# Normalizing the head outputs instead of the softmax rows, and adding the sample's value pages on GpSimd

## The chip, the cores and the metric

The kernel runs on one core of a Trainium2 chip. The metric is the time on the device of one execution, in microseconds (us). Before the change it was 2890.0 us as the median of three runs, from 2884.14 to 2896.01. Engines are called PE (TensorE), DVE (VectorE), ACT (ScalarE), POOL (GpSimd) and SP (SyncE, which issues most of the DMAs).

## The reference, cut to what matters

A two-layer decoder of width 1024 is run for a prompt of 1024 tokens and for 8 sample rows of one token each, in float32: a gated short convolution and a SwiGLU FFN, then one shared K and V with a log-forget value per head, then attention with 16 heads of 64, its output projection and a second FFN. Only the attention is touched:

```python
def _attend(q, k, v, cum_q, cum_kT, q_pos):
    s = jnp.einsum("bqhd,bkhd->bhqk", q, k).astype(jnp.float32) * ATTN_SCALE
    s = s + jnp.swapaxes(cum_q, 1, 2)[..., None] - cum_kT[:, :, None, :]
    k_pos = jnp.arange(k.shape[1])
    s = jnp.where(k_pos[None, :] <= q_pos[:, None], s, -jnp.inf)
    p = jax.nn.softmax(s, axis=-1).astype(v.dtype)
    return jnp.einsum("bhqk,bkhd->bqhd", p, v)
```

For the prompt, q, k and v have 1024 positions. For the samples there is one query per row, and the keys and values are 512 past positions, gathered as four pages of 128 positions out of a pool, and the new one.

## The kernel before, in words

Every engine has its own program, written out by hand, and every order and wait in it is explicit. A float32 operand of a product is kept as a high part (fp32r) and a low part, and a product is two or three matmul passes.

The prompt's attention is done in pairs of heads: 8 pairs, numbered b, and 8 steps in a pair, st 0 to 7, four for each of its two heads e. A step has 256 query rows as two tiles t of 128, and j = st mod 4 says how far down the sequence they are: `span(st, t)`, the width in keys, is 128*(2j+t+1), and `width(st)` is j+1 groups of 256 keys. The work of a step is a pipeline over the engines:

- PE `scores` (L2385, L2388, with a mask pass L2387): q times k-high and k-low into PSUM banks 0 to 3.
- DVE `maxima` (L1953): adds the forget bias, writes the scores to `ss[j]` in SBUF and gives the row's extreme.
- ACT `exps` (L1360): exponential in place, with the row sum. DVE `inverse` (L1961): `ri` = 1 / row sum.
- POOL `norm` (L910): multiplies both tiles of `ss[j]` by `ri`, in place.
- PE `turn` (L2403): transposes the tiles, 128 by 128, into PSUM bank 4 or 5; ACT `pt_high` (L1367) and DVE `pt_low` (L1966) take the high and low part out, group by group.
- PE `values` (L2419, L2420): v times the transposed weights into bank 6 or 7. ACT `o_take` (L1380) copies the result to `oe[e]`, whose two halves of 64 rows belong together.
- When a head is done, SP's `store_head` (L623) writes one half to DRAM (`o_t`), and POOL's `add_halves` (L916) waits for that to land and adds the other half to it by an accumulating DMA.

On PE, step st does `turn` of st, `scores` of st+3 and `values` of st-1. The loop body over b has steps 2 to 9, and steps 8 and 9 are steps 0 and 1 of the next pair. In the last pair, `o_half` (ACT) and `o_sum` (DVE, L1978) add the halves in SBUF.

Loads for the next pair are issued by SP: `load_qk` (L574, L578, L579: q, k, forget bias; `next_qk`), `load_v` (L583; `next_v`). POOL's `k_split` (L899, L901) makes k-high and k-low of a head, and `scores` of that head's first step waits for it. POOL's queue in the body is: norm 4, k_split of the next pair's head 0, norm 5 to 7, add_halves 0, norm 8, k_split of head 1, norm 9 to 11, add_halves 1. SP's is: next_qk 0, value pages 2 and 3, next_qk 1, next_v 0, store_head 0, the next sample's pages 0 and 1, next_v 1, store_head 1.

There are as many samples as pairs of heads, and sample b's past values are summed in pair b. SP loads a page of `cache_v` (L611, 128x1024, two buffers `vp`), and PE's `sample_page` (L2433, at the end of steps 2, 4, 6 and 8) takes the page as weights, eight blocks, against two columns of the sample's softmax weights `pst`. DVE's `sample_sum` (L2003) adds the four pages' results.

Of the kernel before, what the change touches and what calls it, by code (L numbers as in the profile page):

```python
# [62 lines left out]
SCOL = 256  # L63
HIST = 2
# [102 lines left out]
def build(nc, a):  # L167
    ctx = ExitStack()
    with ctx:
# [16 lines left out]
        class Area:  # L186
# [5 lines left out]
            def put(self, name, shape, dt):  # L192
# [128 lines left out]
        vp = Area(Z_END).put("vp", [P, 2, D], F32)  # L321

# [70 lines left out]
              ("khi", "klo", "sfull", "sdr", "exp", "rinv", "pnorm", "tfull", "pthi", "ptlo", "ofull", "ohalf", "odone")}  # L393
# [4 lines left out]
               "pt", "pst", "pe", "o", "osum", "done")}  # L398
# [31 lines left out]
        def _(sp):  # L430
# [256 lines left out]
        def _(pool):  # L687
# [215 lines left out]
            def norm(b, st):  # L903

                j = st % STEPS
                inverted = pool.to_reg(PAIR * b + st + 1) if not isinstance(b, int) else PAIR * b + st + 1
# [15 lines left out]
            norm(0, 0)  # L922
            sample_rows_out()
            k_split(0, 1)
            for st in range(1, STEPS):
                norm(0, st)
            for m in range(WR):
                low(SLOTS["o"] + m, SLOTS["o"] + m)
            with pool.Fori(0, KB - 1) as b:
# [29 lines left out]
        def _(act):  # L959
# [410 lines left out]
            def o_take(b, st):  # L1370

                e, j = st // STEPS % 2, st % STEPS
                act.wait_ge(at["ofull"], PAIR * b + st + 1)
                if j == 0:

                    act.wait_ge(oe_add[e], 16 * (b + st // PAIR + 1))
                if st == 1:

                    act.wait_ge(sm["osum"], b + 1)
                act.activation(oe[e][:, j * 2 * P:(j + 1) * 2 * P], ps[:, 6 + st % 2, 0:2 * P], ACT.Copy).then_inc(at["odone"], 1)  # L1380
# [36 lines left out]
            for st in range(2, PAIR):  # L1417
                step(KB - 1, st, True)
            o_half(PAIR - 2)

            act.wait_ge(sm["o"], NS * PPB + 2)
# [57 lines left out]
        def _(dve):  # L1479
# [490 lines left out]

            def o_sum(st):
# [6 lines left out]
                dve.tensor_tensor(ost[e * DH:(e + 1) * DH, j * 2 * P:(j + 1) * 2 * P], ps[0:DH, 6 + st % 2, 0:2 * P],  # L1978
                                  otmp[:, st % 2, :], ALU.add).then_inc(at["odone"], 1)

            def step(b, st, last=False):


                for g in range(STEPS):
                    if g < width(st):
                        pt_low(b, st, g)
                    if g in (1, 2) and not (last and st + 3 >= PAIR):
                        maxima(b, st + 3, g - 1)
                if not (last and st + 2 >= PAIR):
                    inverse(b, st + 2)  # L1990
                if last and st >= 2:
                    o_sum(st - 2)

            def sample_sum(b):

                paged = dve.to_reg(PPB * b + PPB + 2) if not isinstance(b, int) else PPB * b + PPB + 2
                apart(dve)
                dve.wait_ge(sm["o"], paged)
                taken = dve.to_reg(2 + PAIR * (b + 1)) if not isinstance(b, int) else 1 + PAIR * (b + 1)
                dve.wait_ge(at["odone"], taken)  # L2000
                for t in range(2):
                    rows = slice(t * DH, (t + 1) * DH)
                    last = dve.tensor_reduce(opast[rows, bass.ds(b, 1), :].rearrange("p a k -> p (a k)"),  # L2003
                                             ps[rows, 7, SCOL:SCOL + PPB * H].rearrange("p (g k t) -> p t k g", g=PPB, t=2)[:, t],
                                             AX, ALU.add)
                last.then_inc(sm["osum"], 1)
# [59 lines left out]
        def _(pe):  # L2066
# [303 lines left out]
            def scores(b, st, t):  # L2370
# [7 lines left out]
                if not (isinstance(b, int) and b == 0 and st == 0):  # L2378
                    pe.wait_ge(at["sdr"], 2 * s - 2 + t + 1)
                q = qa[e][:, (2 * j + t) * P:(2 * j + t + 1) * P]  # L2380
# [10 lines left out]
            def turn(b, st, g):  # L2391
# [4 lines left out]
                if g == 0:  # L2396

                    pe.wait_ge(at["pnorm"], 2 * s + 2)
# [173 lines left out]
```

## Time and profile before

| | |
|---|---|
| median of the runs | 2890.0 us |
| profiled execution: its time / its span | 2894.0 us / 2892.3 us |
| PE busy in the span | 2685.8 us (93%) |
| weight loads (PEld) | 2613.1 us (90%) |
| DVE, ACT, POOL busy | 1147.5, 797.7, 943.6 us |
| granted TensorE clock, mean | 0.959 of full |
| L910 (norm) | POOL, 128 instructions, 222.9 us |
| L2433 (sample pages) | PE, 512 instructions, 62.0 us |

The span is divided among engines by what they were busy with; PE's matmuls overlap, so that its busy time includes latency. "Granted clock" is the share of full speed that TensorE was allowed in a stretch. An "idle" or "wait" entry gives how long an engine did nothing ahead of an instruction and what ended that. The attention lies between 1560 and 1942 us from the start; the rest is projections and FFNs (L2069 to L2071), on which PE is busy nearly all of the time.

### The profile page before, as it was taken

The page shows a single profiled execution, that of the slowest core. Times are in us where ns is not written, and L with a number is a line of the kernel's source. Part 1 is how long each engine was busy: PE and PEld are TensorE (multiplying, and loading weights), DVE is VectorE, ACT ScalarE, POOL GpSimd, SP SyncE. Part 2 cuts the span into 40 slices and gives each one's busy share as a digit, 9 for nine tenths or more (in the row PEclk, how much of TensorE's full clock was granted, in tenths as well). Part 3 has the DMA queues.
Part 4 walks back from the last instruction along what each step waited for, and adds up shares of the span by engine and source line. Part 5 has one row for each costly group of instructions (what it writes and reads, how often), then busy time and mean ns, then how long its engine had stood idle before and what let it go on. Part 6 is the DMA issues. An engine that isn't in the chain of part 4 may idle for free.

```text
span 2892.3 us, 45052 instructions
## 1 busy us (share of the span) xinstructions
PE 2685.8 (93%) x16907; PEld 2613.1 (90%) x16907; DVE 1147.5 (40%) x2224; ACT 797.7 (28%) x1483; POOL 943.6 (33%) x572
## 2 busy tenths in 40 slices
PE   8999969999999999689997898879799999999994
PEld 8999969999999999579996787779799999999993
DVE  2222384322222222862455555553742222222247
ACT  3111143111111111342233555651511111111114
POOL 2212153111112212442324888843521221221222
PEclk9999989999999999799998989989999999999996
DMA  3111101111121111024688555631011111111101
GB/s 112 44 51 44 45 23 44 45 45 45 45 59 45 45 52 44 16 81 148 210 283 260 147 165 153 175 116 37 28 53 52 45 45 48 49 44 45 51 30 59
DMA packets 203059, 225.92 MB, mean 78 GB/s; under 512 B 13223, under 2 KB 168871, under 8 KB 201884
## 3 DMA queue, kind: packets, MB, share of 16 engines
q1 hardware_dynamic: 194748, 190.40, 21.7%
q0 software_dynamic: 8160, 33.30, 3.7%
q8 instruction: 121, 1.98, 0.3%
q14 instruction: 30, 0.25, 0.0%
HBM read 182.43 MB, written 41.26 MB: 77 GB/s over the span
## 4 chain that ended last, share of the span: by engine, by line
PE 78%; DVE 9%; issue 4%; POOL 3%; DMA 3%; ACT 3%; SPq 1%; POOLq 0%; DVEq 0%; ACTq 0%
PE ps L2069 24%; PE ps L2070 24%; PE ps L2071 24%; POOL ss L910 2%; DVE ln_d L1560 2%; PE ps L2403 1%; DVE ln_t L1618 1%; DVE ln_t L1622 1%; DMA o_t<-oe 1%; PE ps L2433 1%; PE ps L2388 1%; DVE x L1723 1%; PE ps L2385 1%; PE ps L2420 1%; PE ps L2419 1%
## 5 line engine op out<-in xcount | busy, mean ns | idle before, releaser
L2069 PE MATMUL ps<-xh,whi 128*128 128x344 f32 x3264 | 1056.2, 324 | 51.1 <-issue 37.9
L2070 PE MATMUL ps<-xl,whi 128*128 128x344 f32 x3264 | 1048.8, 321 | 0.0
L2071 PE MATMUL ps<-xh,wlo 128*128 128x344 f32 x3264 | 1048.4, 321 | 0.0
L723 POOL TENSOR_TENSOR wlo<-wraw,whi 128x1024 fp32r<-128x1024 f32 x196 | 469.1, 2398 | 1589.5 <-ACT whi L974 1589.3
L2069 PEld LDWEIGHTS ps<-xh,whi 128*128 128x128 f32 x3264 | 618.8, 190 | 62.2 <-issue 43.4
L2070 PEld LDWEIGHTS ps<-xl,whi 128*128 128x128 f32 x3264 | 618.9, 190 | 0.2
L2071 PEld LDWEIGHTS ps<-xh,wlo 128*128 128x128 f32 x3264 | 618.9, 190 | 0.0
L2069 PE MATMUL ps<-zh,whi 128*128 128x344 f32 x1440 | 474.7, 330 | 40.0 <-DVE x L1723 26.5
L974 ACT ACTIVATE whi<-wraw 128x1024 fp32r<-128x1024 f32 x196 | 206.5, 1056 | 1057.2 <-DMA wraw<-ffn_w_gu 597.8
L2070 PE MATMUL ps<-zl,whi 128*128 128x344 f32 x1440 | 467.8, 325 | 0.0
L2071 PE MATMUL ps<-zh,wlo 128*128 128x344 f32 x1440 | 465.7, 323 | 0.0
L1704 DVE TENSOR_TENSOR silu<-silu,ps 128x344 f32<-128x344 f32 x126 | 64.6, 513 | 833.9 <-PE ps L2071 833.9
L2069 PEld LDWEIGHTS ps<-zh,whi 128*128 128x128 f32 x1440 | 276.4, 192 | 51.8 <-DVE x L1723 33.5
L1723 DVE TENSOR_TENSOR x<-x,ps 128x344 f32<-128x344 f32 x480 | 243.8, 511 | 175.7 <-PE ps L2071 175.7
L2070 PEld LDWEIGHTS ps<-zl,whi 128*128 128x128 f32 x1440 | 276.4, 192 | 0.8 <-issue 0.2
L2071 PEld LDWEIGHTS ps<-zh,wlo 128*128 128x128 f32 x1440 | 276.6, 192 | 0.0
L910 POOL TENSOR_SCALAR ss<-ss,ri 128x128 f32<-128x128 f32 (+7 forms) x128 | 222.9, 1781 | 33.8 <-DVE ri L1961 33.8
L1966 DVE TENSOR_TENSOR ptl<-ps,pth 128x512 fp32r<-128x512 f32 (+1 forms) x160 | 101.3, 635 | 162.2 <-ACT pth L1367 162.0
L2403 PE MATMUL ps<-ident,ss 128*128 128x128 f32 x576 | 107.3, 312 | 46.2 <-POOL ss L910 40.9
L1367 ACT ACTIVATE pth<-ps 128x512 fp32r<-128x512 f32 (+1 forms) x160 | 88.6, 555 | 167.2 <-PE ps L2403 167.0
L1109 ACT ACTIVATE zh<-silu 128x344 fp32r<-128x344 f32 x126 | 61.2, 486 | 256.0 <-DVE silu L1704 256.0
L2403 PEld LDWEIGHTS ps<-ident,ss 128*128 128x128 f32 x576 | 73.2, 158 | 57.1 <-DVE ptl L1966 30.8
(232 smaller groups left out, 2464.2 us busy)
## 6 DMA issues: line engine op xcount, KB each, us to landing
wraw<-ffn_w_gu SPq DMA_DIRECT2D x88, 512.0 KB, 3.9
wraw<-ffn_w_down SPq DMA_DIRECT2D x44, 512.0 KB, 3.5
kp<-cache_k SPq DMA_DIRECT2D x32, 512.0 KB, 5.3
vp<-cache_v SPq DMA_DIRECT2D x32, 512.0 KB, 4.3
wraw<-a_w_in SPq DMA_DIRECT2D x24, 512.0 KB, 3.7
q_t<-hl POOLq DMA_DIRECT2D x8, 1024.0 KB, 4.7
v_t<-vst POOLq DMA_DIRECT2D x8, 1024.0 KB, 7.1
qa<-q_t SPq DMA_DIRECT2D x32, 256.0 KB, 4.2
```

Of the source, the lines that this page charges most:

```text
L723: pool.tensor_tensor(narrow(wlo[:, s, :], cols), narrow(wraw[:, s, :], cols), f32(narrow(whi[:, s, :], cols)), ALU.subtract).then_inc(w_lo, 1)
L910: pool.tensor_scalar(ss[j][:, t, 0:span(st, t)], ss[j][:, t, 0:span(st, t)], ri[:, j, t:t + 1], None, ALU.mult).then_inc(at["pnorm"], 1)
L974: act.activation(narrow(whi[:, s, :], cols), narrow(wraw[:, s, :], cols), ACT.Copy).then_inc(w_hi, 1)
L1109: act.activation(sl(zh[:, slot, :], c), silu[:, c, :], ACT.Copy).then_inc(s["hi"], 1)
L1367: act.activation(pth[st % 2][:, 4 * P * g:4 * P * g + turned(st, g)], ps[:, 4 + tg % 2, 0:turned(st, g)], ACT.Copy).then_inc(at["pthi"], 1)
L1704: dve.tensor_tensor(silu[:, c, :], silu[:, c, :], ps[:, c, 0:CH], ALU.mult).then_inc(s["hid"], 1)
L1723: dve.tensor_tensor(xm, xm, part, ALU.add).then_inc(s["sum"], 1)
L1966: dve.tensor_tensor(ptl[st % 2][:, 4 * P * g:4 * P * g + turned(st, g)], ps[:, 4 + tg % 2, 0:turned(st, g)], f32(pth[st % 2][:, 4 * P * g: ...
L2069: pe.matmul(out, w_h, m_h, start=start, stop=False)
L2070: pe.matmul(out, w_h, m_l, start=False, stop=False)
L2071: return pe.matmul(out, w_l, m_h, start=False, stop=stop)
L2403: mm = pe.transpose(ps[:, 4 + tg % 2, n * P:(n + 1) * P], ss[j][:, t, k * P:(k + 1) * P], ident[:, :])
```

## The change

The prompt's softmax weights are no longer normalized. `norm` and its semaphore go, and `turn` waits for `exps`. PE transposes `ri`, spread over 128 columns, so that each output column's inverse sum stands on all 128 partitions (`inverse_rows`, into the unused half of bank 6 or 7); ACT copies that out (`r_copy`, in the place of `o_take`), and DVE multiplies it into the head output while taking it out of PSUM (`o_scale`). In the last pair `o_sum` gets a multiplication more.

The samples' value pages are weighted and added on POOL (`sample_values`): a product for the first page, a product and a sum for each other, into `vacc`. PE then sums over the partitions once for each sample (`sample_sum`: eight blocks of `vacc` as weights against a column of ones), and DVE copies eight columns. In POOL's queue `sample_values` stand where `norm` stood, and the first pair's k_split of head 1 goes ahead. In SP's queue `next_qk(b+1, 0)` goes ahead of `store_head(b, 1)`.

```diff
+        vacc = Area(PAGES_AT + 2080).put("vacc", [P, D], F32)
+        rbc = Area(SC_AT + PPB * NS * H * 4).put("rbc", [P, 2, 2 * P], F32)
...
# SP
-            with sp.Fori(0, KB - 1) as b:
-                next_qk(b, 0)
+            def head_pair(b, more):
                 load_v_page(b, 2)
                 load_v_page(b, 3)
                 next_qk(b, 1)
...
                 load_v_page(b + 1, 0)
                 load_v_page(b + 1, 1)
                 next_v(b, 1)
+                if more:
+                    next_qk(b + 1, 0)
                 store_head(b, 1)
+            next_qk(0, 0)
+            with sp.Fori(0, KB - 2) as b:
+                head_pair(b, True)
+            head_pair(KB - 2, False)
...
# POOL
-            def norm(b, st):
...
-                pool.wait_ge(at["rinv"], inverted)
-                for t in range(2):
-                    pool.tensor_scalar(ss[j][:, t, 0:span(st, t)], ss[j][:, t, 0:span(st, t)], ri[:, j, t:t + 1], None,
-                                       ALU.mult).then_inc(at["pnorm"], 1)
+            def sample_values(b, g):
+                probs = pst[:, g, bass.ds(b * H, H)].unsqueeze(2).to_broadcast([P, H, DH])
+                page = vp[:, g % 2, :].rearrange("p (h d) -> p h d", d=DH)
+                total = vacc[:, :].rearrange("p (h d) -> p h d", d=DH)
...
+                pool.wait_ge(vp_in[g % 2], loaded)
+                if g == 0:
+                    pool.wait_ge(sm["osum"], taken)
+                    pool.tensor_tensor(total, page, probs, ALU.mult).then_inc(sm["o"], 1)
+                    return
+                pool.tensor_tensor(page, page, probs, ALU.mult).then_inc(sm["mul"], 1)
+                pool.wait_ge(sm["mul"], made)
+                pool.wait_ge(sm["o"], added)
+                pool.tensor_tensor(vacc[:, :], vacc[:, :], vp[:, g % 2, :], ALU.add).then_inc(sm["o"], 1)
...
             with pool.Fori(0, KB - 1) as b:
-                norm(b, STEPS)
+                sample_values(b, 0)
                 k_split(b + 1, 0)
-                for st in range(STEPS + 1, PAIR):
-                    norm(b, st)
+                for g in range(1, PPB):
+                    sample_values(b, g)
                 add_halves(b, 0)
-                norm(b, PAIR)
                 k_split(b + 1, 1)
-                for st in range(PAIR + 1, PAIR + STEPS):
-                    norm(b, st)
                 add_halves(b, 1)
-            for st in range(STEPS, PAIR):
-                norm(KB - 1, st)
+            for g in range(PPB):
+                sample_values(KB - 1, g)
...
# ACT
-                act.activation(oe[e][:, j * 2 * P:(j + 1) * 2 * P], ps[:, 6 + st % 2, 0:2 * P], ACT.Copy).then_inc(at["odone"], 1)
+            def r_copy(b, st):
+                s = PAIR * b + st
+                act.wait_ge(at["rfull"], s + 1)
+                act.wait_ge(at["odone"], s + 1)
+                act.activation(rbc[:, st % 2, :], ps[:, 6 + st % 2, 2 * P:4 * P], ACT.Copy).then_inc(at["rcopy"], 1)
...
                     if g < width(st):
                         pt_high(b, st, g)
+                    if g == 0 and st >= 1:
+                        r_copy(b, st - 1)
                     if g < 2 and not (last and st + 2 >= PAIR):
                         exps(b, st + 2, g)
                 if last and st >= 2:
                     o_half(st - 2)
-                elif st >= 2:
-                    o_take(b, st - 2)
...
# DVE
+            def o_scale(b, st):
...
+                if j == 0:
+                    dve.wait_ge(oe_add[e], stored_before)
+                dve.wait_ge(at["ofull"], summed)
+                dve.wait_ge(at["rcopy"], spread)
+                dve.tensor_tensor(oe[e][:, j * 2 * P:(j + 1) * 2 * P], ps[:, 6 + st % 2, 0:2 * P], rbc[:, st % 2, :],
+                                  ALU.mult).then_inc(at["odone"], 1)
...
                     if g < width(st):
                         pt_low(b, st, g)
+                    if g == 0 and st >= 2 and not last:
+                        o_scale(b, st - 2)
                     if g in (1, 2) and not (last and st + 3 >= PAIR):
                         maxima(b, st + 3, g - 1)
+                if last and st >= 2:
+                    o_sum(st - 2)
                 if not (last and st + 2 >= PAIR):
                     inverse(b, st + 2)
-                if last and st >= 2:
-                    o_sum(st - 2)
...
# PE
-                    pe.wait_ge(at["pnorm"], 2 * s + 2)
+                    pe.wait_ge(at["exp"], 2 * s + 2)
...
                     pe.wait_ge(at["odone"], PAIR * b + st + 1)
+                    pe.wait_ge(at["rcopy"], PAIR * b + st + 1)
...
+            def inverse_rows(b, st):
+                s, j = PAIR * b + st, st % STEPS
+                pe.wait_ge(at["rinv"], s + 1)
+                if not (isinstance(s, int) and s < 1):
+                    pe.wait_ge(at["rcopy"], s)
+                    pe.wait_ge(at["odone"], s + 1)
+                for t in range(2):
+                    mm = pe.transpose(ps[:, 6 + st % 2, (2 + t) * P:(3 + t) * P], ri[:, j, t:t + 1].to_broadcast([P, P]), ident[:, :])
+                mm.then_inc(at["rfull"], 1)
+            def sample_sum(b):
+                pe.wait_ge(sm["o"], PPB * b + PPB + 2)
+                pe.wait_ge(sm["osum"], b + 1)
                 for k in range(KB):
-                    at_col = SCOL + g * H + 2 * k
-                    mm = pe.matmul(ps[:, 7, at_col:at_col + 2], vp[:, g % 2, k * P:(k + 1) * P],
-                                   pst[:, g, bass.ds(H * b + 2 * k, 2)], start=True, stop=True)
-                mm.then_inc(sm["o"], 1)
+                    mm = pe.matmul(ps[:, 1, VSUM + k:VSUM + k + 1], vacc[:, k * P:(k + 1) * P], one[:, 0:1], start=True, stop=True)
+                mm.then_inc(sm["ofull"], 1)
...
                     if g < width(st):
                         turn(b, st, g)
+                    if g == 0 and st >= 1:
+                        inverse_rows(b, st - 1)
                     if g < 2 and not (last and st + 3 >= PAIR):
                         scores(b, st + 3, g)
+                        if g == 0 and st == PAIR + 1:
+                            sample_sum(b)
...
-                if st >= 2 and st % 2 == 0:
-                    sample_page(b, st // 2 - 1)
```

## Rows read from the trace of the kernel before

**Rows 1.** Busy time by stretch: us, then busy (count) of PE, PEld, DVE, ACT, POOL; clock, DMA share, GB/s.
```profile
1722.00:1766.00 44.00, 39.52 (x280) 34.99 (x280) 24.14 (x62) 24.55 (x61) 34.86 (x23) 0.92 0.59 168
...
1753.00:1755.00 2.00, 2.00 (x9) 1.60 (x8) 1.38 (x3) 1.30 (x3) 0.30 (x1) 0.50 0.70 283
...
1791.00:1793.00 2.00, 1.96 (x19) 1.93 (x18) 1.82 (x6) 1.41 (x5) 2.00 (x2) 1.00 1.05 236
```

**Rows 2.** Chain of work that ended last, 1540 to 1960 us: start, length, what.
```profile
1605.14 1.74 PE ps L2433 x16
...
1790.58 7.42 DMA o_t<-oe
...
1892.96 1.73 PE ps L2433 x16
...
1904.01 4.83 DMA o_t<-oe
```

**Rows 3.** Who waited for whom, 1600 to 1900 us: total, times, longest.
```profile
PE ps L2403 <- POOL ss L910: 30.1, 30, 2.1
PEld ps L2403 <- DVE ptl L1966: 26.6, 38, 2.2
POOL o_t L916 <- DMA o_t<-oe: 25.3, 7, 5.1
```

**Rows 4.** PE in order of time, one head at full clock: start, length, line, work, idle before.
```profile
1785.73 0.64 PE L2403 MATMUL ps<-ident,ss 128*128 128x128 f32 x4
1786.12 0.30 PE L2385 MATMUL ps<-kh,qa 128*128 128x128 f32 x1
...
1788.35 0.65 PE L2403 MATMUL ps<-ident,ss 128*128 128x128 f32 x4 [0.61 <-POOL ss L910]
...
1792.34 1.90 PE L2433 MATMUL ps<-pst,vp 128*128 x16
1795.37 0.65 PE L2403 MATMUL ps<-ident,ss 128*128 128x128 f32 x4 [1.14 <-POOL ss L910]
...
1801.22 0.54 PE L2403 MATMUL ps<-ident,ss 128*128 128x128 f32 x3 [1.09 <-POOL ss L910]
...
1805.42 1.89 PE L2433 MATMUL ps<-pst,vp 128*128 x16
1807.40 0.66 PE L2403 MATMUL ps<-ident,ss 128*128 128x128 f32 x4
```

**Rows 5.** Groups by line with shapes kept apart: busy us, mean ns, idle before.
```profile
L910 POOL TENSOR_SCALAR ss<-ss,ri 128x1024 f32<-128x1024 f32 x16 | 45.5, 2846 | 0.0
L723 POOL TENSOR_TENSOR wlo<-wraw,whi 128x1024 fp32r<-128x1024 f32 x195 | 468.6, 2408 | 1582.5 <-ACT whi L974 1582.3
L743 POOL TENSOR_TENSOR ln_s<-ln_s,ln_q 128x1032 f32<-128x1032 f32 x4 | 11.5, 2878 | 1.4 <-ACT ln_q L1017 1.2
L1380 ACT ACTIVATE oe<-ps 128x256 f32<-128x256 f32 x55 | 20.6, 375 | 0.0
```

**Rows 6.** Groups by line, whole kernel: busy us, mean ns, idle before.
```profile
L1876 DVE TENSOR_TENSOR vst<-ps,vst 128x256 fp32r<-128x256 f32 x32 | 11.6, 414 | 2.1 <-ACT vst L1292 2.1
```

**Rows 7.** POOL in order of time.
```profile
1798.64 0.89 POOL L916 DMA_DIRECT2D o_t<-oe  x1 [3.40 <-DMA o_t<-oe]
...
1800.75 1.32 POOL L899 CAST kh<-kd 128x1024 fp32r<-128x1024 f32 x1
1802.16 2.41 POOL L901 TENSOR_TENSOR kl<-kd,kh 128x1024 fp32r<-128x1024 f32 x1
```

**Rows 8.** SP's queue in order of time: DMA issues.
```profile
1786.76 1.16 SPq L574 DMA_DIRECT2D qa<-q_t  x2
...
1790.58 0.53 SPq L623 DMA_DIRECT2D o_t<-oe  x1
```

**Rows 9.** DMA issues, 1650 to 1900 us: KB each, median us to landing.
```profile
vp<-cache_v SPq DMA_DIRECT2D x23, 512.0 KB, 4.2
o_t<-oe SPq DMA_DIRECT2D x12, 256.0 KB, 4.9
```

More of the change, by code:

```diff
@@ L63 @@
 SCOL = 256
+VSUM = 384
 HIST = 2
@@ L397, in build @@
               ("lgd", "prod", "sc", "even", "qk", "qk2", "col", "tsc", "tlg", "sst", "slf", "soft", "exp", "pn",
-               "pt", "pst", "pe", "o", "osum", "done")}
+               "pt", "pst", "pe", "mul", "o", "ofull", "osum", "done")}
         kp_in = [sem(f"kp_in{g}") for g in range(PPB)]
@@ L921, in _ @@
             store_ktok(KB - 1, 1)
-            norm(0, 0)
+            k_split(0, 1)
             sample_rows_out()
-            k_split(0, 1)
-            for st in range(1, STEPS):
-                norm(0, st)
             for m in range(WR):
                 low(SLOTS["o"] + m, SLOTS["o"] + m)
+            pool.wait_ge(sm["pst"], 1)
+            pool.wait_ge(sm["pn"], 2)
             with pool.Fori(0, KB - 1) as b:
-                norm(b, STEPS)
+                sample_values(b, 0)
                 k_split(b + 1, 0)
-                for st in range(STEPS + 1, PAIR):
-                    norm(b, st)
+                for g in range(1, PPB):
+                    sample_values(b, g)
                 add_halves(b, 0)
-                norm(b, PAIR)
                 k_split(b + 1, 1)
-                for st in range(PAIR + 1, PAIR + STEPS):
-                    norm(b, st)
                 add_halves(b, 1)
-            for st in range(STEPS, PAIR):
-                norm(KB - 1, st)
+            for g in range(PPB):
+                sample_values(KB - 1, g)
             proj_low("o", 2)
@@ L1418, in _ @@
                 step(KB - 1, st, True)
+            r_copy(KB - 1, PAIR - 1)
             o_half(PAIR - 2)
-            act.wait_ge(sm["o"], NS * PPB + 2)
             act.wait_ge(sm["done"], 1)
@@ L1969, in pt_low @@
                                   ALU.subtract).then_inc(at["ptlo"], 1)
+            def o_scale(b, st):
+                s = PAIR * b + st
+                e, j = st // STEPS, st % STEPS
+                spread = dve.to_reg(s + 1)
+                summed = dve.to_reg(s + 1)
+                stored_before = dve.to_reg(16 * (b + 1))
+                apart(dve)
+                if j == 0:
[4 more added lines that the diff above has]
+                                  ALU.mult).then_inc(at["odone"], 1)
             def o_sum(st):
@@ L1977, in o_sum @@
                         dve.wait_ge(oe_add[e2], 16 * KB)
-                dve.tensor_tensor(ost[e * DH:(e + 1) * DH, j * 2 * P:(j + 1) * 2 * P], ps[0:DH, 6 + st % 2, 0:2 * P],
-                                  otmp[:, st % 2, :], ALU.add).then_inc(at["odone"], 1)
+                o = ost[e * DH:(e + 1) * DH, j * 2 * P:(j + 1) * 2 * P]
+                dve.tensor_tensor(o, ps[0:DH, 6 + st % 2, 0:2 * P], otmp[:, st % 2, :], ALU.add).then_inc(at["osum"], 1)
+                dve.wait_ge(at["osum"], st + 1)
+                dve.wait_ge(at["rcopy"], PAIR * (KB - 1) + st + 1)
+                dve.tensor_tensor(o, o, rbc[e * DH:(e + 1) * DH, st % 2, :], ALU.mult).then_inc(at["odone"], 1)
             def step(b, st, last=False):
@@ L1986, in step @@
                         pt_low(b, st, g)
+                    if g == 0 and st >= 2 and not last:
+                        o_scale(b, st - 2)
                     if g in (1, 2) and not (last and st + 3 >= PAIR):
                         maxima(b, st + 3, g - 1)
+                if last and st >= 2:
+                    o_sum(st - 2)
                 if not (last and st + 2 >= PAIR):
                     inverse(b, st + 2)
-                if last and st >= 2:
-                    o_sum(st - 2)
             def sample_sum(b):
-                paged = dve.to_reg(PPB * b + PPB + 2) if not isinstance(b, int) else PPB * b + PPB + 2
+                summed = dve.to_reg(b + 1) if not isinstance(b, int) else b + 1
                 apart(dve)
[L1998 to L2006, printed above, removed]
+                dve.wait_ge(sm["ofull"], summed)
+                dve.tensor_copy(opast[:, bass.ds(b, 1), :].rearrange("p a k -> p (a k)"),
+                                ps[:, 1, VSUM:VSUM + KB]).then_inc(sm["osum"], 1)
             for st in range(3):
@@ L2379, in scores @@
                     pe.wait_ge(at["sdr"], 2 * s - 2 + t + 1)
+                if st == PAIR - 2 and t == 0:
+                    pe.wait_ge(sm["osum"], b + 1)
                 q = qa[e][:, (2 * j + t) * P:(2 * j + t + 1) * P]
```

24 lines of the change are left out of this document (9 added, 15 removed).

## The prediction

> **What bounds the kernel now.** The stretches come first, because the change touches one stage only. In the attention no engine is full [rows 1]: in 44 us PE is busy for 39.5 us, POOL 34.9, ACT 24.6, DVE 24.1. PE is the nearest to a bound, POOL second, so the question is which of them waits for which. The chain of waits gives the beat. The value-page matmuls that close steps 4 and 8 stand in it, the first at 1605.14 us and the last at 1892.96 us [rows 2], with 13 half-pairs between them: 287.8 / 6.5 = 44.3 us for a pair of heads. The list of waits says what PE waited for in the 300 us from 1600 to 1900 (6.8 pairs): 30.1 us for POOL's norm and 26.6 us (weight loads, mostly short) for DVE's low parts [rows 3]. POOL in turn lost 25.3 us waiting for a head's store to land [rows 3]. PE in order of time splits a half-pair [rows 4]. From 1785.73 to 1807.40 are 21.7 us at full clock: two pages of 1.9, waits for POOL of 0.61, 1.14 and 1.09, and 15.0 us of everything else, small waits for DVE among it. So a pair is 30.1 us of other PE work, 7.6 of pages, 4.4 of waits for POOL (30.1 / 6.8), and 2.2 that are left, which I put down to the clock: most windows are granted 1.00 (2.4 GHz), as 1791 to 1793, but 1753 to 1755, which follows a wait for POOL, has 0.50, that is 1.2 GHz [rows 1].
>
> **The change, part by part, for one pair.**
>
> *Pages off PE.* Four groups of 16 instructions at 1.9 us go [rows 4]: -7.6 us. One group of 16 of the same kind (eight blocks, two instructions each) comes: +1.9 us.
>
> *Inverse rows on PE.* 16 transposes of 128x128. In the trace four of them and the next matmul are 0.39 us apart (1785.73 to 1786.12, [rows 4]), so 0.10 us each: +1.6 us. The trace doesn't show one whose weights are a single column spread out; from nothing (hidden in a wait) to 0.3 us each, 0 to 4.8 us a pair. I take 1.6, since the shape is the same.
>
> *Norm off POOL.* Its 28 us a pair go (222.9 us by 8) and with them PE's 4.4 us of waits. What is late next is the loop bank 4/5 -> ACT -> DVE -> the same bank: those 26.6 us in 300 are weight-load waits that partly overlap matmuls. They stand inside my 30.1 us, but the pages at the ends of steps 2, 4, 6 and 8 gave the last groups of a step 1.9 us to drain. The step with four groups ends on PE before its last groups are copied out; I put 0.35 us for each such end and as much again for the longer queues of ACT and DVE: +1.4 us a pair (between 0 and 4.4, the wait that goes).
>
> *ACT.* `r_copy` has the shape of `o_take`, 0.375 us [rows 5], eight of each: 0. It is moved ahead of `exps`, so the second group's copy is 0.4 us later in each step, and the next step's first group 0.4 us earlier. It waits for PE's inverse rows, which stand right behind the turn that ACT has just waited for. Behind it are `exps` for two steps on, with a step to spare.
>
> *DVE.* Eight `o_scale` of 128x256 from PSUM; the nearest row has that shape, 414 ns [rows 6]: 3.3 us; two small reductions become one copy. DVE goes from 24.1 to about 27.3 us of a pair. It lies in DVE's waits for ACT, and costs 0 beyond the queue term above. Its new wait, for the add of the pair before (`oe_add`), would hold up every low part behind it; by the schedule below that add lands some 3 us into the pair's step 1 and is first asked for some 5 us in, so 0.
>
> *POOL.* In the place of norm: four products and three sums of 128x1024. The nearest row is a subtraction of that size, 2408 ns [rows 5]; no row has a product with a broadcast operand. A sum of 1032 all in float32 took 2878 [rows 5]. I take 2.4 (the one-row size match with 195 instances), with 2.9 as the other end: 16.8 to 20.3 us. Dependent pairs cost 0.1 between them, so a later page is 4.9 us. POOL's sum falls from 35 us to 16.8 + two `k_split` + two issues = 26 us, but its order has longer waits in it now.
>
> *The Trainium skill against it.* The row says 2.41 us for 1024 elements of two inputs. The Trainium skill (GPSIMD Engine Reference, Performance versus the Vector engine) says some 2.6 cycles per element there, and advises against GpSimd for elementwise work; that would be, as an estimate by that page, 2.2 us and a bit for dispatch, and the trace agrees. The same page (When to use GPSIMD) has one-input operations near line rate, which as an estimate is 0.85 us for 1024; norm's one-input rows say 2.85 [rows 5], and the measurement decides. By the page the norm that goes would be a third as heavy, and POOL would be busier after than before.
>
> *The order, step 9 to step 9.* Let T be the start of PE's step 9 (step 1 of the next pair). SP issues next_v and, now ahead of the store, next_qk: by the same sequence at 1786.76 to 1790.58 [rows 8] that is 3.8 us, so `store_head(b,1)` goes out at T+4.0; `o_scale` of step 7 is done earlier. A store behind such loads landed in 7.4 us [rows 2], against a median of 4.9 [rows 9]: T+11.5. POOL: `add_halves` 1.0, T+12.5; first page 2.4, T+14.9; `k_split` 3.8 (1800.75 to 1804.57, [rows 7]), T+18.7; three pages of 4.9, T+33.4. A page's load (4.2 us, [rows 9]) is asked for a page ahead and hidden. Meanwhile SP stands at page 3 until page 1 is added, T+23.6. Only then come next_qk, next_v and `store_head(b,0)`: out at T+27.9, landed at T+35.3. `add_halves` T+36.3, and `k_split(b+1, 1)` T+40.1. Step 9's first scores need that about 0.5 us after the step's start: 39.6.
>
> *PE's side:* 30.1 + 1.9 + 1.6 + 1.4 = 35.0 at full clock; I leave 1.5 of the 2.2 for the clock, since waits remain: 36.5 us. The first `k_split` (18.7) comes as PE reaches its scores (half of 36.5 and 0.5), so costs nothing. The second costs a stall x after T, and the next one is 39.6 - 36.5 - x: the mean period is (36.5 + 39.6) / 2 = 38.05 us. So 6.2 us saved per pair, of the 7.6 + 4.4 = 12.0 that go.
>
> *Seven loop turns:* -43.7 us. *The ends:* the last pair saves 5.7 on pages and pays 0.8 for inverse rows and about 1 for `o_sum`'s second operation. Its stall for the last add, 4.8 us [rows 2], stays. POOL's pages for it end before PE does. With that, -4. Sum -48: the profiled execution 2894.0 would be 2846, and the median, 4 lower before, 2842.
>
> **Rivals.**
>
> *A, the forecast:* POOL's chain and PE share the period, 2842. Chance 0.45.
>
> *B, PE alone sets the beat.* If stores land in the median 4.9 us, each add is 2.5 us earlier, the second `k_split` falls before step 9, and with short waits the clock stays up: 34.0 us a pair, 10.3 x 7 + 5 = 77, so 2813. For it: POOL's sum is 26 us. Against: the 7.4 us landing is in the chain. Chance 0.22.
>
> *C, the waits come back elsewhere.* PE's 4.4 us turn into waits for low parts, or POOL's operations are 2.9 us and the stores land later: then little beyond the pages is saved (7.6 - 1.9 - 1.6 = 4.1 a pair), 29 + 3 = 32: 2858. For it: 26.6 us in [rows 3] already. Chance 0.20.
>
> *D, nothing moves:* DVE's in-order queue (`o_scale` waiting for the row copy or for the add) takes about what was won: 2885. Chance 0.07.
>
> *E, slower by the clock.* The pages are 7.6 us of matmuls with no waits in them, and 1.6 us of transposes come. If PE is granted 1.2 GHz for much of the pair, 35.0 us of work at a mean clock of 0.70 is 50.0 us: +40 over seven turns, less 4, 2926. It decides at 35.0 / 44.3 = 0.79; the stretch of before has 0.92 [rows 1], and its low windows follow waits, which get fewer. The Trainium skill (TensorE: Matmul & The Clock Gate, PE-mode transpose) says that the full clock does not engage for transposes; here transposes stand between matmuls at 1.00, and by that rule this rival would be the likely one. Chance 0.06.
>
> **The numbers.** About 0.5% (14 us) is what a measurement of this kernel can tell from no change. Faster: A, B and C, 0.87; within: D, 0.07; slower: E, 0.06. The range leaves out E, D and the outer part of B: 2810 to 2874.
>
> **What would show it.** Right: the beat of a pair near 38 us; no wait of turns for POOL; PE waiting 1 to 2 us a pair on `k_split` of head 1, at step 1 of a pair; POOL still waiting for both stores of a pair, each landing 7 us after its issue; products and sums of 2.4 us; DVE near 27 us a pair. B: no wait on `k_split`, 34 us. C: waits on DVE low parts well over 4 us a pair. D: DVE idle ahead of `o_scale`. E: a granted clock under 0.8 in the attention. A product with a broadcast over 3.5 us each would put the chain past 43 us and the period near 40; beyond that the forecast is wrong in its main term.

## The result and the profile after

The changed kernel took 2848.95 us as the median of four runs (2847.24 to 2854.25), the kernel before 2893.01 us beside it (four runs, 2884.14 to 2898.62). The ratio is 0.9854 with a 95% interval of 0.9824 to 0.9884: 44 us, 1.5%, less. A second set of four runs had a median of 2848.82. The profiled execution took 2854.25 us, with a span of 2852.5.

From the first scores matmul of the prompt's attention to the first matmul of the output projection the kernel before needed 382.2 us (1560.6 to 1942.8), the changed one 338.5. So the whole gain lies in the stage that was touched: 43.7 us. (The two profiled executions are 39.8 us apart. Outside this stage the profiles of this case took 2504.6 to 2516.9 us, without order, so that the rest is scatter.) In the loop the start of the k-low subtraction of head 1 marks each pair. From 1614.28 to 1844.65 us are six pairs, 38.4 us a pair; by the same mark the kernel before had 44.0. The prediction's 44.3 went by the page matmuls. So a turn saved 5.6 to 6.0 us, by the mark that is taken (6.0 at the border of steps 8 and 9), seven turns 39 to 42, and between 1.5 and 5 us are left for the ends.

The busy time of each engine over the whole kernel (the first part of the page), then by stretch (us; PE, PEld, DVE, ACT, POOL busy; granted clock, DMA share, GB/s):

```profile
PE 2649.5 (93%) x16651; PEld 2577.8 (90%) x16651; DVE 1169.1 (41%) x2280; ACT 798.4 (28%) x1491; POOL 840.0 (29%) x500
```

```profile
1640.00:1820.00 180.00, 166.30 (x1184) 147.94 (x1184) 126.03 (x330) 117.47 (x289) 104.07 (x60) 0.92 0.71 198
1729.12:1767.49 38.37, 36.62 (x260) 32.65 (x260) 27.45 (x72) 24.75 (x60) 23.23 (x14) 0.91 0.70 191
1772.00:1774.00 2.00, 2.00 (x11) 2.00 (x11) 0.00 (x0) 0.00 (x0) 0.00 (x0) 0.50 1.01 250
```

The second line of the three is one pair, k-low to k-low, and answers to the 44 us of [rows 1]: PE has 36.6 us of work for 38.4, DVE 27.5 (forecast 27.3), ACT as before, POOL 23.2 where it had 34.9. The last line stands 2 us behind a wait of PE, and the clock is at half there, as it was at 1753 us in [rows 1].

The list of waits, 1590 to 1860 us (engine, line, released by: total us, times, longest), answers to [rows 3]:

```profile
POOL o_t L936 <- DMA o_t<-oe: 93.6, 14, 11.5
...
PE ps L2414 <- POOL kl L911: 18.8, 8, 5.5
...
PEld ps L2432 <- DVE ptl L1978: 5.0, 15, 0.3
```

The 30.1 us for norm are gone, and so is most of the 26.6 us that the weight loads waited for DVE's low parts. In their place PE waits for `k_split` of head 1 (L911), and POOL for the stores of both heads.

### The profile page after: what moved, and what is told of

Read it like the earlier page. It is cut to its first block, busy times and chain, and to the rows that moved or that the text cites. A ratio compares the mean times of both kernels' runs of the same rounds, so it can differ in the third digit from the quotient of the medians.

```text
span 2852.5 us, 44492 instructions
## 1 busy us (share of the span) xinstructions
PE 2649.5 (93%) x16651; PEld 2577.8 (90%) x16651; DVE 1169.1 (41%) x2280; ACT 798.4 (28%) x1491; POOL 840.0 (29%) x500
## 4 chain that ended last, share of the span: by engine, by line
PE 78%; DVE 9%; issue 4%; DMA 3%; ACT 2%; POOL 2%; SPq 1%; POOLq 0%; DVEq 0%; ACTq 0%
PE ps L2095 24%; PE ps L2096 24%; PE ps L2097 24%; DMA o_t<-oe 2%; DVE ln_d L1572 2%; DVE ln_t L1630 1%; DVE ln_t L1634 1%; PE ps L2432 1%; DVE x L1735 1%; PE ps L2417 1%; PE ps L2414 1%; DVE ln_s L1580 1%; DMA ncb<-ccum 1%; ACT ln_y L1071 1%; PE ps L2450 1%
## 5 line engine op out<-in xcount | busy, mean ns | idle before, releaser
L2095 PE MATMUL ps<-zh,whi 128*128 128x344 f32 x1440 | 475.1, 330 | 38.7 <-DVE x L1735 25.2
L2414 PE MATMUL ps<-kh,qa 128*128 128x512 f32 (+1 forms) x192 | 80.6, 420 | 38.0 <-POOL kl L911 33.7
L2432 PE MATMUL ps<-ident,ss 128*128 128x128 f32 x576 | 100.7, 298 | 4.1 <-DVE ptl L1978 4.1
L1119 ACT ACTIVATE silu<-ps 128x344 f32<-128x344 f32 x120 | 52.9, 451 | 182.4 <-PE ps L2097 182.2
```

The source lines that it names most:

```text
L2095: pe.matmul(out, w_h, m_h, start=start, stop=False)
L2414: pe.matmul(out, q, kh[e][:, k0:k1], start=True, stop=False)
L2432: mm = pe.transpose(ps[:, 4 + tg % 2, n * P:(n + 1) * P], ss[j][:, t, k * P:(k + 1) * P], ident[:, :])
```

## The experiments

Four kernels of the first set ran beside a before of 2893.6 us, four of the second beside 2890.6, four of the third beside 2892.9. "Beat" is the time from k-low to k-low of head 1 over the six pairs (44.0 before, 38.4 after the change), "stage" the stretch from the first scores matmul to the output projection (382.2 and 338.5). A difference of one or two us in the stage is not much: the changed kernel, profiled again as `e12_change_again`, had a stage of 336.3 and a beat of 37.9.

**One half of the change at a time.** `e1_norm_alone` keeps the change but has the value pages on PE, each with its DVE reduction:

```diff
# POOL
-                for g in range(1, PPB):
-                    sample_values(b, g)
...
# PE
+                if st >= 2 and st % 2 == 0:
+                    pe.wait_ge(at["sdr"], 2 * (PAIR * b + (st + 3 if not (last and st + 3 >= PAIR) else PAIR - 1)) + 1)
+                    sample_page(b, st // 2 - 1)
```

The edit brings one thing of its own: the pages' results stand in bank 1, where scores stand too, so PE waits for DVE's maxima ahead of a page (2.4 us in the 280 from 1600).

> Only the normalization part of the change; the value pages stay matmuls on TensorE (four groups of 1.9 us a pair, results in bank 1). POOL has only k_split and the adds. Theory 1 (PE and POOL's store-add-k_split chain share the period of a pair): POOL's chain ends early, SP is not held at a page, so PE alone sets the beat: 35.0 - 1.9 + 7.6 = 40.7, with the clock about 42 us a pair against 44.3 before and 38.4 with the whole change; about 18 us faster than before. Rival 2 (the 4.4 us of waits for norm are the gain, the pages give nothing): beat 38 to 39 us, as fast as the whole change, 44 us. Rival 3 (the waits come back as waits for low parts): 44 us a pair, no gain.

Measured: 2880.18 us (ratio 0.9947, 0.993 to 0.9964), a beat of 41.8 and a stage of 369.4. That is the beat that the first theory gave, though 13 us came of the 18 that it forecast. From 1640 to 1820 us:

```profile
1640.00:1820.00 180.00, 169.79 (x1289) 150.58 (x1289) 115.78 (x305) 106.63 (x261) 38.73 (x27) 0.99 0.63 171
```

POOL is nearly empty (38.7 of 180 us), PE never waits for it, and the clock is 0.99. Net of the inverse rows, which this kernel has too, norm's going was worth 2.2 us a pair and no more. The list of waits, 1600 to 1880 us, has one line that the account of the prediction needs further down:

```profile
PEld ps L2409 <- DVE ptl L1951: 7.5, 19, 0.5
```

`e2_pages_alone` keeps norm as before and puts the pages on POOL between the norms:

```diff
+                norm(b, STEPS + 1)
+                sample_values(b, 1)
+                norm(b, STEPS + 2)
+                norm(b, STEPS + 3)
                 add_halves(b, 0)
                 norm(b, PAIR)
+                sample_values(b, 2)
...
```

> Only the page part of the change: the norm stays on POOL, the pages are weighted and added there too, PE sums once for each sample. POOL's work in a pair becomes 28 (norm) + 15 (four products of 1.9, three sums of 2.4) + 7 + 2 = 52 us, above the 44.3 us of a pair. Theory 1: POOL sets the beat, 52 us or more a pair, about 56 us slower than before. Rival 2 (PE's busy time counts): 5.7 us a pair are saved, 40 us faster than before.

Measured: 2990.24 us (1.0338, 1.0317 to 1.0359), a beat of 56.7. Two of its pairs by stretch, and what PE waited for from 1620 to 1840 us:

```profile
1690.00:1803.50 113.50, 75.05 (x464) 66.12 (x464) 48.40 (x122) 50.34 (x120) 101.09 (x60) 0.80 0.46 129
```

```profile
PE ps L2431 <- POOL ss L912: 60.1, 19, 6.4
```

POOL has 50.5 us of work a pair and is 89% busy; `turn` waits for norm (L912). The expectation (52 us or more a pair, 56 us slower) left out POOL's own waits; it came out low by 4 to 5 us a pair, and by 41 us in all. The two halves don't add: -13 us alone, +97 us alone, -44 together. POOL has room for the pages only because norm has left it.

**The chain on POOL.** `e3_no_page_work` leaves the arithmetic of pages 1 to 3 out, waits and transfers kept:

```diff
-                pool.tensor_tensor(page, page, probs, ALU.mult).then_inc(sm["mul"], 1)
+                pool.tensor_tensor(page[:, 0:1, 0:1], page[:, 0:1, 0:1], probs[:, 0:1, 0:1], ALU.mult).then_inc(sm["mul"], 1)
```

> The changed kernel with the products and sums of pages 1 to 3 of every sample cut to one column each, so the past values of the samples are not summed; all waits, loads and PE work stay. It takes 13 us a pair off POOL. Theory 1: the second k_split comes some 6 us before PE asks for it, the stall x of 2 to 3 us goes, the beat falls from 38.4 to 35 to 36 us, 17 to 20 us faster than the change. Rival 2 (the landing of head 0's store alone sets k_split, whatever POOL does before): 38 us, no difference. Rival 3 (PE's handshake with ACT and DVE is the bound): 38 us, and no wait for k_split is left.

`e4_extra_sub` does the opposite: the k-low subtraction of head 1 is done twice.

```diff
-                k_split(b + 1, 1)
+                k_split(b + 1, 1, True)
```

> The changed kernel with the low part of head 1's keys computed twice in each k_split of the loop: 2.36 us more on POOL, right on the chain to PE. Theory 1 (period = mean of PE's time and the chain, since the chain starts at the turn before the stall): +1.2 us a pair, +8 us in all. Rival 2 (POOL's chain alone is the period): +2.4 a pair, +16 us. Rival 3 (PE bound, POOL has slack): 0.

Measured (two runs each): 2826.04 us (0.977, 0.9745 to 0.9795) and a beat of 35.2 for the first, 23 us below the change where 17 to 20 were expected; 2861.85 us (0.9894, 0.9869 to 0.9919) and a beat of 39.2 for the second. The 2.4 us that were added to the chain came back as 0.8 us a pair and 6.8 us in the stage, and against the second profile of the changed kernel as 1.2 and 9.0. In the theory of a shared period half of it should, in the rival all of it; the trace is on the theory's side, and the table of periods further down shows both parts. The runs (+13 us) lie between the theory's 8 and the rival's 16, and the time outside the stage differs by up to 12 us from profile to profile, so they don't decide it.

**Three cuts of the same wait, each without taking work away.** `e5_k1_first` lets POOL split k before it waits for the first head's store:

```diff
-                add_halves(b, 0)
                 k_split(b + 1, 1)
+                add_halves(b, 0)
```

> The changed kernel with one swap in POOL's order: k_split of head 1 goes ahead of the add of head 0. Theory 1 (PE's wait hangs on store, landing, add, k_split): k_split may start when the fourth page is added and when head 1's q and k have landed. In the trace of the change the pages end at 1761.9 us, the loads are out at 1757.2 and land some 7 us later, and k_split starts at 1766.1; so the chain gets only 2 us shorter, the period half of that: -1 a pair, -6 to -7 us. Rival 2 (k_split waits for nothing but the store's landing): 4.2 us shorter, -2 a pair, -15 us. Rival 3 (PE is the bound): 0.

`e6_store_first` puts SP's store of head 1 back ahead of the loads of the next q and k:

```diff
+                store_head(b, 1)
                 if more:
                     next_qk(b + 1, 0)
-                store_head(b, 1)
```

> The changed kernel with SP's order as it was before: head 1's store ahead of the next pair's q and k loads. Theory 1: the store goes out some 3 us earlier and lands in some 4 us instead of 8, so the add ahead of the first page comes 6 us earlier, with it everything on POOL; the second k_split comes before PE asks: the beat falls from 38.4 to 35 or 36, -17 us. The move that was part of the change cost that. Rival 2 (the earlier q and k loads are what the first k_split needs): k_split of head 0 becomes late, 0 or slower, +7 us.

`e7_sum_early` lets PE do the sample's sum while it would wait for `k_split`:

```diff
                         if g == 0 and st == PAIR + 1:
+                            pe.wait_ge(at["sdr"], 2 * (PAIR * b + st + 3) - 1)
                             sample_sum(b)
+                        scores(b, st + 3, g)
```

> The changed kernel with PE's sum over a sample's weighted pages moved ahead of the scores that wait for k_split, inside step 9. Theory 1: it fills the wait; the wait gets shorter by its 1.9 us (3.0 as measured, at 1.2 GHz), the period by half of that: -1 to -1.5 a pair, -7 to -10 us, and the granted clock is no lower. Rival 2 (the order within a step is nothing to PE): 0. Rival 3 (its new wait for DVE's maxima stands in the way): slower by 3 us or more.

Measured: e5 2836.0 us (0.9816, 0.9799 to 0.9834), beat 36.4; e6 2841.96 us (0.9831, 0.9815 to 0.9848), beat 36.7; e7 2840.27 us (0.9829, 0.9812 to 0.9845), beat 36.5. e7 did as expected (9 us less than the change), in the beat a little better. e5 gave 2.0 us a pair, about what the rival had: by its number alone it would have decided the other way. Two things in its trace explain it within the theory. The chain became some 2.8 us shorter, more than I had counted, since the wait for the store went with the add (the table below); and the granted clock rose, from 0.92:

```profile
1640.00:1820.00 180.00, 165.83 (x1214) 147.34 (x1213) 128.81 (x336) 118.90 (x288) 114.86 (x66) 0.95 0.72 204
```

Half of 2.8, and 0.6 us of PE's side, half of which shows, are 1.7 us. So a shorter wait seems to pay twice, as time and as clock; e5 alone doesn't separate the two. e6 fell short: 7 us for the 17 that were expected. Its store lands sooner, but POOL's next waits come up behind it (DMA issues, then waits, 1640 to 1820 us):

```profile
o_t<-oe SPq DMA_DIRECT2D x10, 256.0 KB, 5.3
```

```profile
POOL kh L909 <- DMA ncb<-ccum: 9.9, 5, 2.9
PE ps L2414 <- POOL kl L911: 4.8, 2, 2.5
POOL vacc L926 <- DVE opast L2031: 5.1, 2, 3.5
```

The 5.3 us are a median of two kinds. The five stores of head 0, which still stand behind loads, took 6.6 to 7.4 us; the five of head 1, which the edit moved, 3.1 to 4.1, after 7.5 to 8.4 in the changed kernel. But the first page (L926) now waits in some turns until DVE has taken the sum before, and the split of head 0 waits for the loads that had been ahead of the store.

**The whole wait.** `e8_pool_order` takes both store waits out of the chain: POOL adds head 1 of the pair before only after the next pair's first `k_split`, and head 0 after both.

```diff
...
                 sample_values(b, 0)
                 k_split(b + 1, 0)
+                if not first:
+                    add_halves(b - 1, 1)
                 for g in range(1, PPB):
                     sample_values(b, g)
-                add_halves(b, 0)
                 k_split(b + 1, 1)
-                add_halves(b, 1)
+                add_halves(b, 0)
...
+            add_halves(KB - 2, 1)
```

> The changed kernel with POOL's order rewritten: first page, k_split of head 0, only then the add of the pair before's head 1; pages 1 to 3, k_split of head 1, and then the add of head 0. No k_split stands behind a store any more. Theory 1: no wait for k_split is left, the beat is PE's alone, 35 us as with the pages' work left out (35.2 measured), -22 us. Rival 2 (the adds come later and now hold up DVE, which may not overwrite a head's output before them): waits ahead of DVE's scaling, 37 to 38 us, -5 us.

Measured: 2824.12 us (0.9775, 0.9759 to 0.9791), a beat of 34.3, a stage of 310.2. From 1640 to 1820 us, by stretch and by waits:

```profile
1640.00:1820.00 180.00, 172.73 (x1320) 152.37 (x1319) 140.03 (x365) 129.30 (x317) 120.47 (x68) 1.00 0.76 215
```

```profile
POOL kh L909 <- DMA ncb<-ccum: 30.8, 11, 4.8
POOL vacc L926 <- DVE opast L2038: 25.1, 5, 7.7
...
PEld ps L2439 <- DVE ptl L1985: 6.6, 18, 1.0
...
PE ps L2421 <- POOL kl L911: 0.6, 2, 0.4
```

PE's wait for `k_split` fell from 9.3 us in this stretch to 0.6, and the clock is at 2.4 GHz throughout. POOL has 60 us in which it does nothing, and next to none of it reaches PE. No line of the list has POOL waiting for a store: the adds stand where their stores have long landed. This is the state that rival B forecast, PE alone, reached in another way.

**What is left.** `e9_order_and_sum` is e8 with e7's edit. `e10_psum_osum` is e8 with the last pair's halves added in PSUM, so that DVE's multiplication has one operand in SBUF instead of two. `e11_all_three` has all of them.

```diff
-                dve.tensor_tensor(o, ps[0:DH, 6 + st % 2, 0:2 * P], otmp[:, st % 2, :], ALU.add).then_inc(at["osum"], 1)
+                both = ps[0:DH, 6 + st % 2, 0:2 * P]
+                dve.tensor_tensor(both, both, otmp[:, st % 2, :], ALU.add).then_inc(at["osum"], 1)
...
-                dve.tensor_tensor(o, o, rbc[e * DH:(e + 1) * DH, st % 2, :], ALU.mult).then_inc(at["odone"], 1)
+                dve.tensor_tensor(o, both, rbc[0:DH, st % 2, :], ALU.mult).then_inc(at["odone"], 1)
```

> The rewritten POOL order and the early PE sum together. Theory 1: in the run with the new POOL order alone the beat is 34.3 us a pair, the granted clock 1.00, and PE waits for no k_split; the early sum has nothing left to fill: 0 against that run, within 3 us of 2824. Rival (the two add up, as they hit different waits): -7 us, 2817.

> The rewritten POOL order, and in the last pair DVE adds the two halves back into PSUM and multiplies from there, so that no DVE operation of the attention reads two operands from SBUF. In the change the multiplication of 64x256 took 0.42 us as a rule, but 1.07 and 2.27 us when a POOL operation was running, and ended 0.3 us after it. If DVE waits there for POOL (two operands from SBUF), all eight take 0.4 us now, and the last pair is 2 to 3 us shorter: 2821 to 2822. Rival (the long ones are something else, as a late semaphore in the profile): they stay, 0.

> New POOL order, early sum and the last pair's multiplication from PSUM. Theory: the sum of the three, of which the early sum gives 0: 2820 to 2822, 27 us (1%) faster than the change, 70 us (2.4%) faster than before.

> The changed kernel itself, on the same chip and beside the same runs of before as the last three, as their base: 2849 within 5 us.

Measured: e9 2822.91 us (0.9766, 0.9745 to 0.9786), the same as e8: a cover for a wait is worth nothing when the wait has gone. e10 2823.95 (0.9755, 0.9736 to 0.9773): the long multiplications went (below), but 2 to 3 us can't be told from none. e11 2821.88 (0.9752, 0.9736 to 0.9767, five rounds) is the lowest by its median, and not to be told from e8. It is 27 us below the change and 71 us, 2.5%, below the kernel before. `e12_change_again`, the changed kernel itself, took 2848.82.

## Why the prediction was right, step by step

**The period.** The forecast was a chain through POOL that needs 39.6 us and PE's own 36.5, which share the period: 38.05, measured 38.4. PE in order of time at four starts of step 9, in the changed kernel: `inverse_rows` (L2463) near the start of the step, the scores matmul that waits (L2414; in brackets the idle time before it), the sample's sum (L2472):

```profile
1652.88 0.38 PE L2463 MATMUL ps<-ident,ri 128*128 128x128 f32 x2
1654.70 0.32 PE L2414 MATMUL ps<-kh,qa 128*128 128x128 f32 x1 [1.44 <-POOL kl L911]
1655.04 1.90 PE L2472 MATMUL ps<-one,vacc 128*128 128x1 f32 x16
...
1689.21 0.38 PE L2463 MATMUL ps<-ident,ri 128*128 128x128 f32 x2
1693.32 0.47 PE L2414 MATMUL ps<-kh,qa 128*128 128x128 f32 x1 [3.73 <-POOL kl L911]
1693.94 3.51 PE L2472 MATMUL ps<-one,vacc 128*128 128x1 f32 x16
...
1730.54 0.38 PE L2463 MATMUL ps<-ident,ri 128*128 128x128 f32 x2
1731.63 0.32 PE L2414 MATMUL ps<-kh,qa 128*128 128x128 f32 x1 [0.71 <-POOL kl L911]
1731.97 2.33 PE L2472 MATMUL ps<-one,vacc 128*128 128x1 f32 x16
...
1767.71 0.38 PE L2463 MATMUL ps<-ident,ri 128*128 128x128 f32 x2
1769.98 0.32 PE L2414 MATMUL ps<-kh,qa 128*128 128x128 f32 x1 [1.89 <-POOL kl L911]
1770.33 3.07 PE L2472 MATMUL ps<-one,vacc 128*128 128x1 f32 x16
```

A period less the wait at its start is PE's side; a period plus the wait at its end is the chain. So from 1652.88 to 1689.21 are 36.33 us, PE's side 36.33 - 1.44 = 34.9, the chain 36.33 + 3.73 = 40.1. Worked out in that way for six periods of each kernel (means, us; for e8 the five from 1648.65 to 1818.48, at clock 1.00 and with waits of 0.1 in the mean, so that no chain counts; its first, ahead of them, took 37.6 at clock 0.91):

| | period | PE's side | chain |
|---|---|---|---|
| forecast | 38.05 | 36.5 | 39.6 |
| changed kernel | 38.1 | 35.9 | 40.6 |
| the same, profiled again (e12) | 38.1 | 36.1 | 39.9 |
| e4, 2.4 us added to the chain | 39.6 | 35.8 | 43.0 |
| e5, split ahead of the add | 36.5 | 35.3 | 37.7 |
| e8, no store wait ahead of a split | 34.0 | 33.9 | - |

(From step to step instead of from k-low to k-low the means differ by up to 0.5 us, because the first and the last wait differ.) That the period is the mean of the two other columns proves nothing, since one wait is taken off and the next put on. The test is e4: it put some 2.4 us on the chain (0.7 us is what two profiles of one kernel differ by) and none on PE's side, and the period moved by 1.5. Had the chain alone set the period, the period would have moved by 2.4. Where a turn ends without a wait, as every second one of e5 does, the chain ended earlier than its column says. That the waits can come long and short in turn belongs to the mechanism: a late start of the step leaves the next split more time. The four above do (1.4, 3.7, 0.7, 1.9), and in e4 all seven (7.0, 1.5, 4.7, 2.4, 4.7, 2.5, 4.2); the last two of the changed kernel, 1.5 and 5.5, follow no such order.

The forecast's two parts were off to either side, PE's by -0.6 us and the chain by +1.0 (-0.4 and +0.3 in e12), so that their mean came out nearer than they did. The wait that it gave PE, 1.6 us a pair, was 2.6 in the mean of seven.

**The links of the chain.** The chain that ended last, with T = 1730.2 us, and POOL's queue in order of time:

```profile
1734.57 7.45 DMA o_t<-oe
...
1758.17 6.70 DMA o_t<-oe
...
1766.06 1.36 POOL kh L909
1767.49 2.36 POOL kl L911
```

```profile
1742.65 0.84 POOL L936 DMA_DIRECT2D o_t<-oe  x1 [11.16 <-DMA o_t<-oe]
1743.28 2.15 POOL L926 TENSOR_TENSOR vacc<-vp,pst 128x1024 f32<-128x1024 f32 x1
1746.49 2.40 POOL L911 TENSOR_TENSOR kl<-kd,kh 128x1024 fp32r<-128x1024 f32 x1
...
1759.55 2.39 POOL L931 TENSOR_TENSOR vacc<-vacc,vp 128x1024 f32<-128x1024 f32 x1
1765.50 0.86 POOL L936 DMA_DIRECT2D o_t<-oe  x1 [3.56 <-DMA o_t<-oe]
```

The store of head 1 goes out at T+4.4 (forecast 4.0) and lands at T+11.8 (11.5 worked out as T+4.0 plus 7.4). The first `k_split` ends at T+18.7 (18.7), the pages at T+31.7 (33.4). The store of head 0 goes out at T+28.0 (27.9) and lands at T+34.7 (35.3), and the second `k_split` ends at T+39.6 (40.1). The pages came early, yet the chain gained little, because it ran through SP there: the store of head 0 ended last, not the last page. The pages aren't out of the chain, though. SP's queue stands at page 3 until page 1 is added, as forecast, and the store comes behind it; that fits what leaving their arithmetic out gave in e3, 3.1 us a pair. e5 and e8 show it from the other side: with every product and sum still there, a store wait less ahead of `k_split` (e5) or none (e8) shortens the period.

**Durations.** Groups with shapes kept apart, 1590 to 1860 us (busy us, mean ns, idle before):

```profile
L2432 PE MATMUL ps<-ident,ss 128*128 128x128 f32 x498 | 85.6, 293 | 2.7 <-DVE ptl L1978 2.7
L931 POOL TENSOR_TENSOR vacc<-vacc,vp 128x1024 f32<-128x1024 f32 x22 | 52.6, 2390 | 1.7
L928 POOL TENSOR_TENSOR vp<-vp,pst 128x1024 f32<-128x1024 f32 x22 | 41.9, 1906 | 1.0 <-DMA vp<-cache_v 0.5 <-POOL vacc L931 0.4
L1995 DVE TENSOR_TENSOR oe<-ps,rbc 128x256 f32<-128x256 f32 x54 | 22.4, 415 | 0.0
L2463 PE MATMUL ps<-ident,ri 128*128 128x128 f32 x110 | 22.5, 289 | 0.0
...
L1392 ACT ACTIVATE rbc<-ps 128x256 f32<-128x256 f32 x55 | 21.0, 381 | 0.0
```

Sums were 2.39 (forecast 2.4), the products 1.91, `o_scale` 415 ns (414), `r_copy` 381 ns (375), and an inverse row costs what any transpose of its size does (289 and 293 ns with latency).

**The term that was mis-sized.** I had added 1.4 us a pair for handshakes with DVE's low parts. The waits for them fell instead, from 26.6 us in 300 to 5.0 in 270 for the weight loads, and PE at full clock needs 33.9 us a pair (e8), not 35.0. e1 shows what they hung on: there norm alone is gone and the pages are still on PE, and the waits are down to 7.5 us in 280 (its line above). So most of that wait went when norm did, without the pages' going; how norm brought it about is not shown. (e2, which keeps norm, has little of it too, 3.1 us in 220, but there PE waits for norm so long that DVE's parts are ready.) The other way goes PE's side in the changed kernel, 35.9 - 33.9 = 2.0 us a pair above e8's, where 1.5 was taken for the clock. I put it down to the clock, 0.92 against 1.00; short waits for DVE may be in it.

**The rivals.** B was one reordering away: forecast at 34.0 us a pair and 77 us less, e8 has 34.3 a pair, a stage 72.0 us shorter and runs that are 67 us below its before. Two things about B were luck. Its 34.0 stood 1.0 below the prediction's own sum for PE alone, 35.0, without a reason. And the way that it named, stores that land sooner, doesn't lead there: the median of 4.9 us in [rows 9] was one of two kinds (in the kernel before, head 1's stores took 2.9 to 3.0 us and head 0's 6.8 to 8.5), and e6, with head 1's store at 3.1 to 4.1, has a beat of 36.7. C's waits for low parts didn't appear. D is out, for `o_scale` causes no wait in the list. E is out: the transposes came and the pages went, and the stage's clock stayed 0.92 and rose to 1.00 in e8. The Trainium skill (TensorE: Matmul & The Clock Gate, PE-mode transpose) has no full clock for transposes; this trace disagrees for a stream in which they stand between other matmuls, e8 having 1.00 over 180 us of it.

**The ends** gave between 1.5 and 5 us, and 4 was forecast; the marks don't tell it closer. Inside them two things went otherwise. The stall for the last add (4.8 us in [rows 2]), which was to stay, is gone from the chain. And in the last pair, 1845 to 1905 us, PE has a new wait:

```profile
PE ps L2463 <- DVE ri L1973: 8.4, 3, 3.5
```

DVE's inverse of a step stands behind `o_sum` in its queue, and PE's inverse rows need it. A smaller part of it may be `o_sum`'s long multiplications, which the last section shows: without them the same wait is still 8.3 us (e10) and 7.2 (e11); with them it is 8.1 in e12 and 10.7 in e8. No run takes the order alone.

## What to carry to other kernels

When work moves to an in-order queue, sum up both loops that meet there. If an engine waits for a chain once a turn, and the chain was started ahead of the engine's wait before, the mean of the two sets the beat: about half of what is cut from either shows, and the clock can give back some more. Look in such a queue for instructions that wait for a fresh transfer (here the add behind a store) and let them stand behind whatever another engine needs next: that reordering was worth 25 us here, over half as much as the rewrite itself. A median over transfers that stand at two places of a queue hides both: look at each place. And try the halves of a change apart: here one alone was 97 us slower, and only the other made room for it.

## What the runs showed of the hardware

**A wait costs clock too.** Behind a wait of 1.44 us the sample's sum took 1.90 us as at full clock; behind 1.89 us it took 3.07, behind 3.73 us 3.51 (the fence on PE above); the granted clock was 0.50 in the 2 us from 1772, just behind the wait of 1.89. One wait of 0.71 us was followed by 2.33, so the length of the wait alone doesn't tell it.

**VectorE held up by GpSimd.** `o_sum`'s multiplication of 64x256, both operands in SBUF, usually takes 0.42 us. In the last pair of the changed kernel two of eight were longer. DVE, then POOL, in order of time:

```profile
1859.63 1.07 DVE L2009 TENSOR_TENSOR ost<-ost,rbc 64x256 f32<-64x256 f32 x1
...
1867.21 2.27 DVE L2009 TENSOR_TENSOR ost<-ost,rbc 64x256 f32<-64x256 f32 x1
```

```profile
1858.06 2.35 POOL L931 TENSOR_TENSOR vacc<-vacc,vp 128x1024 f32<-128x1024 f32 x1
...
1866.87 2.34 POOL L931 TENSOR_TENSOR vacc<-vacc,vp 128x1024 f32<-128x1024 f32 x1
```

Each ends 0.3 us after the POOL sum that ran when it began, and so does the one of 2.57 us in e8. With one operand in PSUM (e10) the longest of the eight was 0.418 us. The Trainium skill (SBUF — State Buffer, "SBUF: two separate sides") says that such a two-operand VectorE instruction and a GpSimd instruction on SBUF shut each other out of a shared port for their whole length; the trace agrees.

**A broadcast operand is cheaper on POOL.** A product of 128x1024 whose second operand repeats each value over 64 columns took 1.91 us, a sum of two full operands of the same size 2.39. That one is a product and the other a sum hardly makes it: at 128x344, both operands full, a product took 1.02 us (L969) and a sum 1.02 (L753).

**A store behind loads.** From 1640 to 1820 us head 1's stores of 256 KB landed in 8.2 us (median of five, 7.5 to 8.4) when next_qk's loads were issued just ahead of them, and in 3.4 (3.1 to 4.1) when they were issued behind them (e6).
